# The tensors of a two-block transformer kernel placed in another order in SBUF

## The chip, the cores and the metric

The kernel runs on one core of a Trainium2 chip. The metric is the device time of one execution in microseconds (us); the median of three is 3204.19 us.

## The reference

Two transformer blocks of two layers each, on a sequence of 256 tokens with model width 2048 (batch 1), in float32. The first block has an even layer (latent attention, blocked causal attention, attention over a memory of 256 rows) and an odd one (windowed attention, dilated attention, memory attention). The second has two layers that each run a top-k sparse attention, a gated causal convolution of width 31 over 1024 channels, and a stick-breaking attention, merged by gates. Every layer has the same frame, in which nearly all multiplications lie:

```python
h = rms_norm(x, norm_g) @ w_in            # 256 x 2048 by 2048 x (some 7,000 to 18,064)
...
x = x + (y * silu(gate)) @ w_out          # block 1; block 2: x + merged @ w_out
```

After each block x is normalised by rms_norm with a gain. The weights are read once, some 557 MB in all.

## The kernel before

**The weight products.** Every product with a weight matrix is cut into "gemms" of up to 512 output columns, and each gemm into "fills" of 256 rows of the weight. There are 1088 fills. A fill f goes through five steps. SP's queue loads 2 x 512 float32 for each of 128 partitions (512 KB) into `raw[f % 4]`, in pieces of 2048 bytes (step `raw`). ScalarE copies it as float32r (`wh[f % 4]`, step `hi`, line 118). VectorE subtracts that from `raw` and gets the remainder (`wl[f % 4]`, step `lo`, line 121). TensorE multiplies (step `mm`, line 103): the activations lie transposed in a high and a low half (Hh and Hl, or Yh and Yl), and for each of two row blocks and two halves of the tokens it issues three matmuls, high x high, high x low, low x high: twelve per fill. `wh` and `wl` are the moving operand with up to 512 columns, a 128 x 128 piece of H or Y is the stationary one. The sums are in PSUM (`gp`, two buffers), and ScalarE and VectorE take them out.

**The other work.** Attention heads, transposes (`ident` is the identity for them; line 106), softmaxes, the convolution (31 `tap` steps on VectorE per channel block, line 126, reading `glu`, then `mean` and `var` on TensorE with the constant `ones`), and the norms are small steps that run between fills.

**What is placed where.** `place` (line 306) allocates SBUF with a stack. The compiled program of the kernel before starts it at byte 16,512 of each partition and rounds each tensor's length up to 32 bytes. Names that the text uses: X is the residual stream, H and Y the pairs of transposed activations, Z a second pair (`Yh2`, `Yl2`), M (`merged`) the sum of the branches, of which `glu`, `cv` and `csq` of the convolution are parts, G the attention regions (`ones`, `tri`, `kiT` lie at its ends), `nat`, `tmp` and `st` rings of buffers, `cc` the convolution's columns, `gc` (`gcols`) the gains. Y, `mkT` and `mv` are allocated in an `ExitStack` called `first` that ends before Z and M are allocated, so Z and M lie over them: these tensors share bytes, in time one after the other.

**What sets the order.** A planner sketches every step of every engine with an estimated duration from the operation's element count, then builds each engine's order by simulating it: steps become ready when what they wait for is done, rings give buffers, and `urgency` ranks what is ready. The order found is what each engine runs, with waits on semaphores. It is computed when the program is built.

Of the kernel before, what the change touches and what calls it, by code (L numbers as in the profile page):

```python
# [5 lines left out]
F = mybir.dt.float32  # L6
R = mybir.dt.float32r
# [288 lines left out]
class Program:  # L296
# [7 lines left out]
    def sb(self, name, shape, dt=F, ctx=None):  # L304
        return (ctx or self.ctx).enter_context(self.nc.sbuf_tensor(name, shape, dt))

    def place(self):
        nc, sb = self.nc, self.sb
        self.ident = sb("ident", [128, 128])
        self.cc = sb("cc", [128, 272])  # L310
        self.small = sb("small", [128, 64])
        sb("pad", [128, 16])
        self.X = sb("X", [128, 2, 2048])
        H = (sb("Hh", [128, 16, 256], R), sb("Hl", [128, 16, 256], R))
        self.raw = [sb(f"raw{i}", [128, 2, 512]) for i in range(RAW)]
        self.wh = [sb(f"wh{i}", [128, 2, 512], R) for i in range(SPLIT)]
        self.wl = [sb(f"wl{i}", [128, 2, 512], R) for i in range(SPLIT)]
        self.G = sb("G", [128, 2, 4608])
        self.nat = Ring(self.plan, [sb(f"nat{i}", [128, 2, 512])[:] for i in range(2)])
        self.tab = sb("tab", [128, 2, 256])  # L320
        self.tmp = Ring(self.plan, [sb(f"tmp{i}", [128, 512])[:] for i in range(5)])
        with ExitStack() as first:
            Y = (sb("Yh", [128, 20, 256], R, first), sb("Yl", [128, 20, 256], R, first))
            self.mkT = sb("mkT", [128, 1024], F, first)
            self.mv = sb("mv", [128, 2, 512], F, first)
        Z = (sb("Yh2", [128, 16, 256], R), sb("Yl2", [128, 16, 256], R))
        self.M = sb("merged", [128, 2, 2048], F)
        self.masks = sb("masks", [128, 3, 384])
        self.gcols = sb("gc", [128, 102])
        self.st = Ring(self.plan, [sb(f"st{i}", [128, 8])[:] for i in range(10)])  # L330
        self.gp = [self.ctx.enter_context(nc.psum_tensor(f"gp{i}", [128, 2, 512], F)) for i in range(2)]
        banks = [self.ctx.enter_context(nc.psum_tensor(f"bk{i}", [128, 512], F))[:] for i in range(4)]
        self.bank = Ring(self.plan, banks)
        self.pairs = {"H": [H, H, H, Z], "Y": [Y, Y, Z, H]}
        M = self.M[:, :, :].rearrange("p t c -> p (t c)")
        self.glu = M[:, 0:8 * 286].rearrange("p (c t) -> p c t", t=286)
        self.cv = self.glu[:, :, 30:286]
        self.acc_tap = [M[:, 2304:2560], M[:, 2560:2816]]
        self.csq = M[:, 2304:3328].rearrange("p (c t) -> p c t", t=256)
        self.cvar = [M[:, 3584:3840], M[:, 3840:4096], M[:, 2304:2560]]  # L340
        self.region = []
        for i in range(2):
            d = {k: self.G[:, i, 1024 * n:1024 * n + 1024] for n, k in enumerate("qkvg")}
            d["pe"] = self.G[:, i, 4096:4608]
            self.region.append(d)
        g0, g1 = self.region[0]["pe"], self.region[1]["pe"]
        self.memnat = self.G[:, 1, 0:4096].rearrange("p (t c) -> p t c", t=2)
        self.gfin = self.G[:, 0, 0:2048]
        self.kpe = self.cc[:, 0:256]
        self.swk, self.swv = g1, g0  # L350
        self.kiT, self.ones = g1[:, 0:256], g1[:, 288:416]
        self.wi = g1[:, 256:288].rearrange("p (t h) -> p t h", t=2)
        self.work, self.tri = g0[:, 0:384], g0[:, 384:512]
        self.acc, self.strict = self.masks[:, 1, :], self.masks[:, 2, :]
        s = self.small
        self.rs, self.rsh, self.rm, self.rq, self.rk = s[:, 0:2], s[:, 2:4], s[:, 4:6], s[:, 20:22], s[:, 22:24]
        self.sum_x, self.sum_q, self.sum_kv, self.sum_m = s[:, 8:16], s[:, 16:18], s[:, 18:20], s[:, 48:56]
        self.zero = s[:, 40:41]
# [1674 lines left out]
```

How the kernel before makes its waits and increments, by code:

```python
    def wait_ge(self, sem, value):  # L81
        if sem is None:
            return
        if self.e is None:
            self.plan.step.waits += [(sem, k) for k in value]
        elif self.seen.get(id(sem), 0) < value:
            self.e.wait_ge(sem, value)
            self.seen[id(sem)] = value
# [699 lines left out]
    def load_mem2():  # L788
        e.wait_ge(*P.p_in.at(("y", 3, 2)))
        e.dma_start(P.memnat, m).then_inc(*P.s_mem2.up("mem", 16))
# [1 line left out]
    def raw(f):  # L792
        gm, j = P.fills[f]
        if f:
            e.behind("raw", f - 1)
        else:
            e.behind("load_mem", 3)
        if f == RAW:
            e.behind("load_x", 3)
        if f >= RAW:
            e.wait_ge(*P.v_lo.at(f - RAW))
        elif f == 1:
            e.wait_ge(*P.s_id.at("id"))
            e.wait_ge(*P.s_rows.at(*range(8)))
        k = 256 * j
        src = gm.w[k:k + 256, gm.c0:gm.c0 + gm.n].rearrange("(t p) n -> p t n", p=128)
        e.dma_start(P.raw[f % RAW][:, :, 0:gm.n], src).then_inc(*P.s_raw[f % RAW].up(f, 16))
# [10 lines left out]
    def load_constants():  # L818
        for n in range(4):
            e.wait_ge(*P.s_x[n].at("x"))
        e.dma_start(P.masks[:, :, :], I["c_masks"][0:3].rearrange("m p c -> p m c")).then_inc(*P.s_masks.up("m", 16))
        e.dma_start(P.tab[:, :, :], I["c_tab1"]).then_inc(*P.s_tab.up("t", 16))
        e.dma_start(P.small[:, 24:40], I["od_sinks"].broadcast_to([128, 16])).then_inc(*P.s_sinks.up("s", 16))
# [29 lines left out]
    def pad(l):  # L853
        if l:
            e.wait_ge(*P.p_in.at(("m", 0, 14)))
        else:
```

## Time and profile before

| what | value |
|---|---|
| median of three executions | 3204.19 us (3203.88 to 3207.12) |
| the profiled execution, its own time | 3207.12 us |
| its span, first to last instruction | 3205.3 us |
| mean granted clock of TensorE, as a share of 2.4 GHz | 0.995 |
| TensorE, VectorE, ScalarE busy | 99%, 62%, 50% |
| SP's transfers, share of sixteen DMA engines | 58.2% |
| moved from and to HBM, mean | 176 GB/s |

The profile is of one execution. An engine's busy share is a mean over the span; TensorE's is made of matmuls whose ends are modelled, so two that follow one another overlap in it, and the time of one step is the distance between two starts. The chain that ended last goes back from the last instruction to what released each one, and says whose time the span is made of.

### The profile page before, as it was taken

Reading aid. Unit: us, or ns where it says so; the run is one execution under the profiler, and the core shown is the slowest. Engines: PE = TensorE matmul, PEld = TensorE weight load, DVE = VectorE, ACT = ScalarE, POOL = GpSimd, SP = SyncE. Lnnn points to the kernel's source line nnn. Section 1 sums busy time; section 2 is a strip of 40 time slices with the busy share of each in tenths; the row PEclk is TensorE's granted clock in tenths of the full one; section 3 lists DMA queues with packets and bytes.
Section 4 is the critical chain, followed back from the end, with each engine's and each line's share of the span. In section 5 each row is a group of like instructions: output and inputs, shape, how many; then the busy total and the mean of one; then the engine's idle time right before and its main releaser. Section 6 shows DMA issues by size and latency. Waiting matters only on the chain.

```text
span 3205.3 us, 38474 instructions
## 1 busy us (share of the span) xinstructions
PE 3164.4 (99%) x15199; PEld 2656.7 (83%) x15199; DVE 1981.0 (62%) x2987; ACT 1600.4 (50%) x2254; POOL 14.2 (0%) x30
## 2 busy tenths in 40 slices
PE   8999999999999899999999999999999999999997
PEld 7888888888988788888888888888888888888886
DVE  5555455555554699976554555558999655555554
ACT  6654454555554544556544444454454645444443
POOL 0000000000000000000000000000000000000000
PEclk9999999999999999999999999999999999999999
DMA  6546656555466555555566666566555566666664
GB/s 230 173 135 173 171 194 185 177 156 154 143 191 205 153 179 164 166 156 165 170 191 191 188 196 194 181 188 177 168 171 164 152 177 179 195 201 194 193 186 140
DMA packets 300559, 566.14 MB, mean 177 GB/s; under 512 B 18088, under 2 KB 36814, under 8 KB 299868
## 3 DMA queue, kind: packets, MB, share of 16 engines
q1 hardware_dynamic: 298384, 557.65, 58.2%
q0 software_dynamic: 1648, 5.92, 0.5%
q8 instruction: 120, 1.97, 0.3%
q14 instruction: 59, 0.48, 0.0%
q10 hardware_dynamic: 348, 0.12, 0.0%
HBM read 561.52 MB, written 2.10 MB: 176 GB/s over the span
## 4 chain that ended last, share of the span: by engine, by line
PE 98%; DVE 1%; ACT 1%; ACTq 0%; issue 0%; DMA 0%; POOL 0%; DVEq 0%
PE gp L103 90%; PE bk L103 5%; PE bk L106 3%; DVE X L126 0%; ACT bk L118 0%; ACTq L162 0%; DMA tmp<-in_conv_ln_b 0%; ACT L115 0%; DVE X L121 0%; POOL tmp L162 0%; DVE Yl L126 0%; ACT gp L118 0%; DVE tmp L138 0%; DVE wl L121 0%; ACT G L118 0%
## 5 line engine op out<-in xcount | busy, mean ns | idle before, releaser
L121 DVE TENSOR_TENSOR wl<-raw,wh 128x1024 fp32r<-128x1024 f32 (+3 forms) x1088 | 1287.5, 1187 | 955.7 <-ACT wh L118 954.3
L118 ACT ACTIVATE wh<-raw 128x1024 fp32r<-128x1024 f32 (+3 forms) x1088 | 1119.7, 1032 | 1347.0 <-PE gp L103 1338.8
L103 PE MATMUL gp<-wh,Hh 128*128 128x512 f32 (+3 forms) x2400 | 926.3, 386 | 0.1
L103 PE MATMUL gp<-wh,Hl 128*128 128x512 f32 (+3 forms) x2400 | 912.6, 380 | 0.0
L103 PE MATMUL gp<-wl,Hh 128*128 128x512 f32 (+3 forms) x2400 | 911.9, 380 | 0.0
L103 PE MATMUL gp<-wh,Yh 128*128 128x512 f32 (+2 forms) x1952 | 763.1, 391 | 0.0
L103 PE MATMUL gp<-wh,Yl 128*128 128x512 f32 (+2 forms) x1952 | 755.5, 387 | 0.0
L103 PE MATMUL gp<-wl,Yh 128*128 128x512 f32 (+2 forms) x1952 | 755.3, 387 | 0.0
L103 PEld LDWEIGHTS gp<-wh,Hl 128*128 128x128 f32 x2400 | 451.7, 188 | 86.5
L103 PEld LDWEIGHTS gp<-wh,Hh 128*128 128x128 f32 x2400 | 452.2, 188 | 82.7 <-issue 1.3
L103 PEld LDWEIGHTS gp<-wl,Hh 128*128 128x128 f32 x2400 | 452.3, 188 | 81.4
L103 PEld LDWEIGHTS gp<-wh,Yl 128*128 128x128 f32 x1952 | 367.1, 188 | 74.6
L103 PEld LDWEIGHTS gp<-wl,Yh 128*128 128x128 f32 x1952 | 367.5, 188 | 71.7
L103 PEld LDWEIGHTS gp<-wh,Yh 128*128 128x128 f32 x1952 | 367.4, 188 | 71.3
L126 DVE SCALAR_TENSOR_TENSOR merged<-merged,cc 128x256 f32<-128x256 f32 x480 | 202.0, 478 | 0.0
L118 ACT ACTIVATE nat<-gp,small 128x512 f32<-128x512 f32 (+3 forms) x228 | 133.9, 632 | 136.3 <-PE gp L103 136.1
L103 PE MATMUL bk<-G 128*128 128x128 f32 (+3 forms) x408 | 73.8, 333 | 0.3 <-DVE st L138 0.2
L103 PEld LDWEIGHTS bk<-G 128*128 128x128 f32 (+1 forms) x408 | 59.9, 189 | 10.9 <-issue 3.0
L118 ACT ACTIVATE tmp<-tmp,st 128x128 f32<-128x128 f32 (+1 forms) x124 | 55.8, 451 | 18.5 <-DVE st L132 18.5
L118 ACT ACTIVATE tmp<-bk 128x384 f32<-128x384 f32 (+1 forms) x110 | 50.8, 494 | 25.2 <-PE bk L106 22.7
L103 PEld LDWEIGHTS bk<-G,tmp 128*128 128x128 f32 x420 | 52.8, 191 | 2.7
L103 PE MATMUL bk<-G,tmp 128*128 128x128 f32 (+1 forms) x420 | 53.0, 273 | 0.0
(118 smaller groups left out, 1247.7 us busy)
## 6 DMA issues: line engine op xcount, KB each, us to landing
raw<-in_w_in SPq DMA_DIRECT2D x560, 512.0 KB, 3.8
raw<-in_ev_w_in SPq DMA_DIRECT2D x104, 512.0 KB, 3.8
raw<-in_od_w_in SPq DMA_DIRECT2D x80, 512.0 KB, 3.7
raw<-in_w_out SPq DMA_DIRECT2D x64, 512.0 KB, 4.0
raw<-in_ev_w_out SPq DMA_DIRECT2D x40, 512.0 KB, 3.6
raw<-in_od_w_out SPq DMA_DIRECT2D x36, 512.0 KB, 4.3
raw<-in_w_b_out SPq DMA_DIRECT2D x32, 512.0 KB, 4.8
raw<-in_w_a_out SPq DMA_DIRECT2D x32, 512.0 KB, 4.8
```

Of the source, the lines that this page charges most:

```text
L103: return self.e.matmul(out, l, r, start=start, stop=stop)
L106: return self.sketch(112) if self.e is None else self.e.transpose(out, in_, ident)
L118: return self.e.activation(out, in_, func, **kw)
L121: return self.sketch(157 + size(a) * 1.042) if self.e is None else self.e.tensor_tensor(out, a, b, op)
L126: return self.e.scalar_tensor_tensor(out=out, in0=a, scalar=s, in1=b, op0=op0, op1=op1)
```

## The change

The change is in `place` alone. It allocates the same tensors in another order and leaves out `pad`, 64 bytes that nothing uses. X comes first; `ident`, `cc`, `small` and `tab` go behind the rings, with `st`, `masks` and `gc` that stood at the end; Z and M get an `ExitStack` of their own, `second`, after which nothing is allocated. The PSUM tensors are allocated before `first` instead of at the end, in their old order.

```diff
     def place(self):
         nc, sb = self.nc, self.sb
-        self.ident = sb("ident", [128, 128])
-        self.cc = sb("cc", [128, 272])
-        self.small = sb("small", [128, 64])
-        sb("pad", [128, 16])
         self.X = sb("X", [128, 2, 2048])
...
         self.nat = Ring(self.plan, [sb(f"nat{i}", [128, 2, 512])[:] for i in range(2)])
+        self.tmp = Ring(self.plan, [sb(f"tmp{i}", [128, 512])[:] for i in range(5)])
+        self.st = Ring(self.plan, [sb(f"st{i}", [128, 8])[:] for i in range(10)])
+        self.ident = sb("ident", [128, 128])
+        self.masks = sb("masks", [128, 3, 384])
+        self.gcols = sb("gc", [128, 102])
+        self.cc = sb("cc", [128, 272])
         self.tab = sb("tab", [128, 2, 256])
-        self.tmp = Ring(self.plan, [sb(f"tmp{i}", [128, 512])[:] for i in range(5)])
+        self.small = sb("small", [128, 64])
+        self.gp = [self.ctx.enter_context(nc.psum_tensor(f"gp{i}", [128, 2, 512], F)) for i in range(2)]
+        banks = [self.ctx.enter_context(nc.psum_tensor(f"bk{i}", [128, 512], F))[:] for i in range(4)]
+        self.bank = Ring(self.plan, banks)
         with ExitStack() as first:
             Y = (sb("Yh", [128, 20, 256], R, first), sb("Yl", [128, 20, 256], R, first))
             self.mkT = sb("mkT", [128, 1024], F, first)
             self.mv = sb("mv", [128, 2, 512], F, first)
-        Z = (sb("Yh2", [128, 16, 256], R), sb("Yl2", [128, 16, 256], R))
-        self.M = sb("merged", [128, 2, 2048], F)
-        self.masks = sb("masks", [128, 3, 384])
-        self.gcols = sb("gc", [128, 102])
-        self.st = Ring(self.plan, [sb(f"st{i}", [128, 8])[:] for i in range(10)])
-        self.gp = [self.ctx.enter_context(nc.psum_tensor(f"gp{i}", [128, 2, 512], F)) for i in range(2)]
-        banks = [self.ctx.enter_context(nc.psum_tensor(f"bk{i}", [128, 512], F))[:] for i in range(4)]
-        self.bank = Ring(self.plan, banks)
+        with ExitStack() as second:
+            Z = (sb("Yh2", [128, 16, 256], R, second), sb("Yl2", [128, 16, 256], R, second))
+            self.M = sb("merged", [128, 2, 2048], F, second)
```

The first byte of each tensor in a partition, worked out from the lengths:

| tensor | bytes | start before | start after |
|---|---|---|---|
| X | 16,384 | 18,432 = 9 x 2048 | 16,512 = 8 x 2048 + 128 |
| Hh, Hl | 2 x 16,384 | 34,816 = 17 x 2048 | 32,896 = 16 x 2048 + 128 |
| raw, wh, wl | 4 x 4096 each | 67,584; 83,968; 100,352 | 65,664; 82,048; 98,432 |
| G | 36,864 | 116,736 = 57 x 2048 | 114,816 = 56 x 2048 + 128 |
| nat, tmp | 2 x 4096, 5 x 2048 | 153,600; 163,840 | 151,680; 159,872 |
| ident | 512 | 16,512 | 170,432 |
| cc | 1088 | 17,024 | 175,968 |
| tab | 2048 | 161,792 | 177,056 |
| Yh (and Z over it) | 20,480 | 174,080 = 85 x 2048 | 179,360 = 1401 x 128 + 32 |
| M | 16,384 | 206,848 = 101 x 2048 | 212,128 = 1657 x 128 + 32 |
| masks | 4608 | 223,232 | 170,944 |

## Rows read from the trace of the kernel before

**Rows 1.** The page, parts 1 and 3: busy us, share, instructions; the SP queue.
```profile
PE 3164.4 (99%) x15199; PEld 2656.7 (83%) x15199; DVE 1981.0 (62%) x2987; ACT 1600.4 (50%) x2254; POOL 14.2 (0%) x30
...
q1 hardware_dynamic: 298384, 557.65, 58.2%
```

**Rows 2.** The page, part 4: the chain that ended last, by engine and line.
```profile
PE 98%; DVE 1%; ACT 1%; ACTq 0%; issue 0%; DMA 0%; POOL 0%; DVEq 0%
PE gp L103 90%; PE bk L103 5%; PE bk L106 3%; DVE X L126 0%; ACT bk L118 0%; ACTq L162 0%; DMA tmp<-in_conv_ln_b 0%; ACT L115 0%; DVE X L121 0%; POOL tmp L162 0%; DVE Yl L126 0%; ACT gp L118 0%; DVE tmp L138 0%; DVE wl L121 0%; ACT G L118 0%
```

**Rows 3.** The same chain in order of time: start, us, what, instructions.
```profile
959.55 87.07 PE gp L103 x384
...
1774.29 250.26 PE gp L103 x1104
```

**Rows 4.** Timeline of TensorE at 1000 us: start, duration, what.
```profile
1000.21 0.39 PE L103 MATMUL gp<-wh,Yh 128*128 128x512 f32 x1
...
1000.89 0.39 PE L103 MATMUL gp<-wh,Yh 128*128 128x512 f32 x1
```

**Rows 5.** Groups by line: busy us, mean ns of one, idle before.
```profile
L103 PE MATMUL gp<-wh,Hh 128*128 128x512 f32 (+3 forms) x2400 | 926.3, 386 | 0.1
...
L103 PE MATMUL gp<-wh,Yh 128*128 128x512 f32 (+2 forms) x1952 | 763.1, 391 | 0.0
...
L103 PEld LDWEIGHTS gp<-wh,Yh 128*128 128x128 f32 x1952 | 367.4, 188 | 71.3
```

**Rows 6.** Timeline of TensorE: first the mean, then the variance's first half.
```profile
1421.59 3.62 PE L103 MATMUL bk<-merged,G 128*128 128x256 f32 x16
...
1430.53 1.89 PE L103 MATMUL bk<-merged,G 128*128 128x256 f32 x8
```

**Rows 7.** Timeline of TensorE in a gemm of 256 columns.
```profile
625.06 0.28 PE L103 MATMUL gp<-wh,Hh 128*128 128x256 f32 x1
625.18 0.28 PE L103 MATMUL gp<-wl,Hh 128*128 128x256 f32 x1
```

**Rows 8.** Groups of weight loads by form: busy us, mean ns, idle before.
```profile
L103 PEld LDWEIGHTS bk<-merged,G 128*128 128x128 f32 x64 | 12.1, 189 | 1.9
...
L103 PEld LDWEIGHTS bk<-cc,G 64*128 64x128 f32 x32 | 4.7, 184 | 3.6 <-issue 2.7
```

**Rows 9.** Line 126 on VectorE: duration ns min/median/max, first and last start.
```profile
L126 DVE SCALAR_TENSOR_TENSOR merged<-merged,cc x480: 464/478/491, 1115.5 to 2482.8; 128x256 f32<-128x256 f32 x160
...
L126 DVE SCALAR_TENSOR_TENSOR Hl<-bk,gc,Hh x48: 472/476/484, 36.0 to 1071.0; 128x256 fp32r<-128x256 f32 x48
```

**Rows 10.** Busy us per stretch: span, PE, PEld, DVE, ACT, POOL; clock, DMA, GB/s.
```profile
2200.00:2500.00 300.00, 300.00 (x1480) 253.77 (x1479) 269.30 (x539) 147.25 (x216) 0.00 (x0) 1.00 0.57 168
```

**Rows 11.** DMA from 1774 to 2024 us: queue (packets, MB, share); issues, us to landing.
```profile
q1 hardware_dynamic: 24809, 47.83, 64.7%
...
raw<-in_w_in SPq DMA_DIRECT2D x56, 512.0 KB, 4.3
...
raw<-in_w_c_out SPq DMA_DIRECT2D x16, 512.0 KB, 5.0
```

**Rows 12.** Waits: engine, line, for what, us in total, times, longest.
```profile
PE bk L106 <- DMA ident<-in_c_ident: 10.6, 1, 10.6
...
ACT wh L118 <- DMA raw<-in_od_w_in: 4.9, 5, 2.0
...
PEld gp L103 <- DVE wl L121: 0.3, 1, 0.3
```

**Rows 13.** Busy us of the first 20 us, columns as in rows 10.
```profile
0.00:20.00 20.00, 7.08 (x27) 6.11 (x28) 6.58 (x16) 14.38 (x33) 0.29 (x5) 1.00 0.83 280
```

**Rows 14.** Busy us in the pause between the blocks, columns as in rows 10.
```profile
1050.00:1055.00 5.00, 1.11 (x5) 1.12 (x6) 3.40 (x9) 2.45 (x6) 0.00 (x0) 0.50 0.38 107
```

**Rows 15.** The chain at the pause's end: start, us, what.
```profile
1059.83 4.46 PE gp L103 x12
```

## The prediction

> **What bounds the kernel now.** I read the page first. TensorE is busy in 99% of the span, VectorE in 62%, and SP's transfers take 58.2% of sixteen DMA engines [rows 1]. A busy share of TensorE proves little alone, since the ends of its matmuls are modelled, so the chain that ended last comes next: 98% of it is TensorE, 90% the one line that issues the split matmuls of the weight products, and VectorE and ScalarE have 1% each [rows 2]. The time is the sum of TensorE's own steps.
>
> How long is one such step? The chain has a stretch of 1104 matmuls and nothing else in 250.26 us: 0.2267 us each; one some 800 us earlier has 384 in 87.07 us, again 0.2267 us [rows 3]. The timeline shows it from start to start: three steps from 1000.21 to 1000.89 [rows 4]. The long stretch runs through all raw and split slots many times, with transfers landing and ScalarE and VectorE reading and writing beside it, and its mean is that of the short one. So other engines' accesses don't slow TensorE's reads today, and new addresses can only change the step itself, or make something else late enough to be waited for.
>
> The groups give the count: 2400 matmuls with H and 1952 with Y, each in three kinds, 3 x 2400 + 3 x 1952 = 13,056 [rows 5]. Most have 512 columns.
>
> **The change, part by part.** It touches no instruction, size, loop, ring or wait. The planner orders steps by names, element counts and ring slots; no address enters it, the rings keep their lengths, and PSUM is laid out as before. Tensors that shared bytes (Z and M over Y, mkT and mv) share the same bytes relative to each other, so no new overlap wants a new wait. The order on each engine stays, and what differs is the byte at which each tensor starts. Five things could cost something.
>
> (1) *Matmuls.* wh, wl and H move from multiples of 2048 bytes to 128 bytes past a multiple of 256. Does TensorE care where a moving operand starts? No row has the split matmul at another kind of start. The nearest is in the convolution. Its mean reads `cv`, whose rows start 120 + 1144c bytes into M, at a different place in a 64-byte block for each of the eight c; its variance reads `csq`, on a multiple of 1024. The mean's 16 passes take 3.62 us, the variance's 8 take 1.89 us [rows 6]. Less the last pass's 0.38 us that is 3.24 / 15 = 0.216 us and 1.51 / 7 = 0.216 us from start to start: odd starts cost nothing that shows. But such a pass of 256 columns takes 0.216 / 256 = 0.84 ns per column, and the split matmul takes 0.120 us for 256 [rows 7], so (0.2267 - 0.120) / 256 = 0.417 ns per column: it reads twice as fast, and the row is near but not the thing itself. I take 0. Upper bound: one column time for each, 13,056 x 0.417 ns = +5.4 us. Lower bound: the same with the other sign, as 0.2267 us is 512 x 0.417 = 0.213 us and 13 ns of fixed part, and nothing proves that no part of it comes from today's starts.
>
> The Trainium skill ("SBUF — State Buffer", Specifications) says that SBUF has lines of 16 bytes and that each crossing to a new one costs something. By that rule the sum stays as well, as every tensor starts on such a line before and after; the mean's operands, half of which start 8 bytes past one, are where this trace could have shown the cost, and 0.216 us against 0.216 us doesn't show it.
>
> (2) *Weight loads from Y and Z.* These move from multiples of 512 to 32 bytes past a multiple of 128. A load takes 188 ns and the next matmul starts 227 ns after the last [rows 5, 4]: 39 ns of cover. The mean's loads, from `ones` at 128 past a multiple of 512, take 189 ns, and those from half the rows 184 ns [rows 8]. With 1 to 4 ns between forms and 39 ns of cover I take 0 for both bounds; without cover 1 ns on each of 5856 would be +6 us.
>
> (3) *VectorE and ScalarE* read and write Y, Z and M at 32 past a multiple of 64. The 480 convolution taps read `glu` at a start that moves by 4 bytes per tap and last 464 to 491 ns, median 478; the same operation and size into Hl, always on a round start, 476 [rows 9]. Were each 13 ns longer (the maximum less the median), that is 6.2 us of VectorE for both layers. In the tightest stretch, 2200 to 2500 us, it is busy for 269 of 300 us while TensorE is busy for all 300 [rows 10]: 31 us of cover for one layer's half. Without cover, +6.2 us. I take 0.
>
> (4) *Weight transfers.* Each 2048-byte piece of `raw` starts 128 past a multiple of 256. In the long stretch SP's transfers occupy 64.7% of the engines for 47.83 MB, 91.2 tiles of 512 KB: 0.647 x 250 / 91.2 = 1.77 us per tile [rows 11], against 12 x 0.2267 = 2.72 us of TensorE. A tile has to become 1.53 times dearer before transfers set the pace. Latency is covered too: `lo` frees the raw slot of tile f - 4 about 2.3 us (ScalarE's 1.06, VectorE's 1.22) after TensorE is done with f - 8, and `hi` can take tile f only once TensorE is done with f - 4. That leaves 4 x 2.72 - 2.3 = 8.6 us for a landing of 4.3 to 5.0 us [rows 11]. ScalarE waits 4.9 us in all for the worst group of raw tiles, and TensorE's loads wait for `lo` 0.3 us [rows 12]. If it had no cover, each 1% on a tile would be 18 ns on 1016 full ones, 18 us. I take 0.
>
> The Trainium skill ("DMA: Bandwidth & Descriptors", How a descriptor splits into AXI transactions) says that transfers are made of transactions that begin at multiples of 256 bytes, so that a descriptor off such a multiple needs one more. It speaks against this change. By it 2048 bytes would take 9 instead of 8, an estimate of 1.77 x 9 / 8 = 2.0 us per tile, still under 2.72, and the sum would be the same; no row of before can show it.
>
> (5) *Start and end.* Only here are transfers close to the bound: they are 0.83 busy in the first 20 us [rows 13], and TensorE waits for ident until 10.6 us [rows 12]. If they got a tenth dearer (my choice) and nothing hid it, the start would be 2 us later, and the last stores a little. I take 0, with 0 and +2 us as bounds.
>
> **Sum.** The profiled execution took 3207.12 us, its span 3205.3 us, so 1.8 us lie around it. 3207.12 + 0 (five times) = 3207.1 us. It is the slowest of the three executions, 2.9 us (0.09%) above their median of 3204.19, so as a median I forecast **3204.2 us**. About 0.2%, 6.4 us, is what a measurement of this kernel can tell from no change.
>
> **Rivals.**
> *The split matmul does mind its start.* For it: no row has it at another start, and it is 90% of the chain. Against: rows 6. With four column times more on each, 13,056 x 1.67 ns = +21.8 us: **3226 us**. It decides from 6.4 / 13,056 = 0.49 ns per matmul on, little more than one column time.
> *Transfers become the bound.* If a tile took twice its time, 3.54 us against 2.72: 0.82 x 1016 = +830 us, **4037 us**. It decides from a factor of 1.53 on. Against it: rows 11; nothing in the trace shows a transfer that slows by so much.
> *The old starts were the worse ones.* Place: the 13 ns of fixed part. With four column times less, 3204.2 - 21.8 = **3182 us**. For it only that the fixed part is there; against it rows 6. It decides from -0.49 ns on.
> *The half clock moves.* After TensorE's pause at 1046.6 us its granted clock is 0.50 of 2.4 GHz, the lower level of 1.2 GHz [rows 14], and twelve matmuls take 4.46 us instead of 2.72 [rows 15]. The pause is a chain of ScalarE and VectorE steps that stays. Without the lower clock some 2 us would come back: **3202 us**, which lies within no change.
>
> **How the numbers follow.** Within 0.2%: 0.88, of which 0.86 is my forecast and 0.02 the half clock. Slower by more: 0.09, of which 0.07 is the matmul that minds its start and 0.02 transfers. Faster by more: 0.03, the old starts. Range: up +5.4 for the column time, +2 for the start and 1.4 for the part of the slow matmul's case just above, giving 3213; down 2 us for the clock and 1 for scatter (the runs lie from 3203.88 to 3207.12), giving 3201. I leave out the full -5.4 us, for which nothing speaks but symmetry. Less than 0.15 is left outside.
>
> **What would show each step right or wrong.** Right: the same number of instructions, the chain at 98% TensorE, long stretches of L103 at 0.2267 us per matmul. (1) is wrong if that quotient is 0.2272 or more, or 0.2262 or less. (2) is wrong if loads from Yh or Yl take over 200 ns while those from Hh keep 188. (3) would show in the taps' 478 ns. (4) would show in SP's share of the DMA engines, 58.2%, and matters only if ScalarE's waits for raw grow past some 10 us. (5) would show in the start of the first weight product. The prediction fails as a whole if the order of steps changed, or if the split matmul's step depends on where its operand starts.

## The result and the profile after

The changed kernel takes 3240.84 us in the median of four executions, beside 3204.69 us for the kernel before on the same chip: a ratio of 1.0111 (95% interval 1.0099 to 1.0124), 36 us or 1.1% slower. I had forecast 3204.2 us and no change; the time lies outside my range of 3201 to 3213 us.

The page of the changed kernel, parts 1 and 4:

```profile
span 3240.7 us, 38474 instructions
...
PE 3199.1 (99%) x15199; PEld 2657.2 (82%) x15199; DVE 1982.5 (61%) x2987; ACT 1601.1 (49%) x2254; POOL 14.2 (0%) x30
...
PE 98%; DVE 1%; DMA 0%; ACT 0%; issue 0%; POOL 0%; SPq 0%; DVEq 0%
```

The counts are those of before, VectorE's and ScalarE's busy times moved by 1.5 and 0.7 us, and TensorE still has 98% of the chain [rows 1, 2]. The matmuls of the two traces follow one another with the same names and forms, all 15,199 of them. So the same steps run in the same order, and TensorE's own steps got longer. Which ones, the chain in order of time tells:

```profile
286.80 29.94 PE gp L103 x132
...
964.83 89.61 PE gp L103 x384
...
1782.91 252.65 PE gp L103 x1104
...
2866.12 255.34 PE gp L103 x1104
```

The first stretch has H as its stationary operand: 29.94 / 132 = 0.2268 us per matmul, the old step. The second has Y: 89.61 / 384 = 0.2334 us, where it was 0.2267 [rows 3]. The two long ones show it again. In the third layer (1782.91) 348 of the matmuls have Z as stationary operand and are slow: 252.65 - 250.26 = 2.4 us is 6.9 ns for each. In the fourth (2866.12) the roles are exchanged, H's lines run on Z, and the other 756 are slow: 5.1 us, 6.7 ns each. So it goes by the bytes from which the stationary operand is read, and the moving operand's new start, which all stretches share, costs nothing.

The groups by form give the count and the sum:

```profile
L103 PE MATMUL gp<-wh,Hh 128*128 128x512 f32 x2176 | 861.4, 396 | 0.0
...
L103 PE MATMUL gp<-wh,Yh 128*128 128x512 f32 x1888 | 754.8, 400 | 0.0
...
L103 PE MATMUL gp<-wh,Yl 128*128 128x384 f32 x32 | 10.8, 336 | 0.0
```

Matmuls of 512 columns with a Y or Z piece: 3 x 1888 = 5664. 5664 x (0.2334 - 0.2268) = 37 us, against a loss of 36 us. The trace's own loads of these pieces didn't get longer: they take 188 ns as before [rows 5].

```profile
L103 PEld LDWEIGHTS gp<-wh,Yh 128*128 128x128 f32 x1952 | 367.6, 188 | 82.4
```

Only the idle time ahead of them grew, from 71.3 to 82.4 us for this kind. And the convolution's mean, which was my measure of an odd start, takes 3.62 us as in [rows 6], although M moved too.

```profile
1428.80 3.62 PE L103 MATMUL bk<-merged,G 128*128 128x256 f32 x16
```

### The profile page after: what moved, and what is told of

Same layout as the page of the kernel before. It is cut to its first block, busy times and chain, and to the rows that moved or that the text cites. A ratio compares the mean times of both kernels' runs of the same rounds, so it can differ in the third digit from the quotient of the medians.

```text
span 3240.7 us, 38474 instructions
## 1 busy us (share of the span) xinstructions
PE 3199.1 (99%) x15199; PEld 2657.2 (82%) x15199; DVE 1982.5 (61%) x2987; ACT 1601.1 (49%) x2254; POOL 14.2 (0%) x30
## 3 DMA queue, kind: packets, MB, share of 16 engines
q1 hardware_dynamic: 298384, 557.65, 57.3%
## 4 chain that ended last, share of the span: by engine, by line
PE 98%; DVE 1%; DMA 0%; ACT 0%; issue 0%; POOL 0%; SPq 0%; DVEq 0%
PE gp L103 90%; PE bk L103 5%; PE bk L106 3%; DVE X L126 0%; DMA G<-in_mem 0%; DMA tmp<-in_conv_ln_b 0%; ACT L115 0%; DVE X L121 0%; POOL tmp L162 0%; DVE Yl L126 0%; ACT gp L118 0%; DVE tmp L138 0%; ACT bk L118 0%; SPq L162 0%; DVE wl L121 0%
## 5 line engine op out<-in xcount | busy, mean ns | idle before, releaser
L103 PE MATMUL gp<-wh,Yh 128*128 128x512 f32 (+2 forms) x1952 | 774.4, 397 | 0.0
L103 PE MATMUL gp<-wh,Yl 128*128 128x512 f32 (+2 forms) x1952 | 766.9, 393 | 0.0
L103 PE MATMUL gp<-wl,Yh 128*128 128x512 f32 (+2 forms) x1952 | 766.8, 393 | 0.0
L103 PEld LDWEIGHTS gp<-wh,Yh 128*128 128x128 f32 x1952 | 367.6, 188 | 82.4
```

The source lines that it names most:

```text
L103: return self.e.matmul(out, l, r, start=start, stop=stop)
```

## The experiments

Each is an edit of one of the two kernels that adds unused bytes. "Distance" is the stationary operand's first byte (H or Y) less the moving one's (wh), modulo 256. It is 0 for both in the kernel before, and H 0, Y 32 in the changed one (179,360 - 82,048 = 97,312 = 380 x 256 + 32). For offsets it is enough to look at the first bytes: wh and wl, the halves of H, Y and Z, and the pieces within them all lie multiples of 256 bytes apart, unless a run says otherwise. Every ratio is to the kernel before, measured beside it.

### Y alone, 32 bytes further

```diff
+        sb("pad_y", [128, 8])
         with ExitStack() as first:
```

> The kernel before with 32 unused bytes ahead of Yh: only Y, mkT, mv, Z, M, masks, gc and st move, by 32 bytes, and all else stays. Theory A (TensorE's stationary operand must start on a multiple of 64 bytes, absolutely): each of the 5664 matmuls of 512 columns with a stationary Y or Z piece takes 0.2333 us instead of 0.2267, +36 us, about 3241 us. Theory B (what counts is the distance between the starts of the moving and the stationary operand): Y stands at 32 from wh's multiple of 64, so +36 us as well. Theory C (the order of the other tensors, ident, cc, tab or masks, or the 128 bytes of H, wh and raw cause it): no change, 3204 us.

Measured: 3239.99 us, ratio 1.0107 (1.0091 to 1.0122).

```profile
285.74 29.94 PE gp L103 x132
...
963.84 89.62 PE gp L103 x384
```

H 0.2268 us, Y 0.2334 us: the whole loss, from moving Y and what lies behind it by 32 bytes in the kernel before. Theory C falls: neither the new order of the small tensors nor the 128 bytes of wh, H and raw have a part in it.

### All big tensors 32 bytes further

```diff
-        sb("pad", [128, 16])
+        sb("pad", [128, 24])
```

> The kernel before with the pad made 96 bytes instead of 64: every tensor from X on moves by 32 bytes, so H, Y, Z, wh, wl and raw all start 32 bytes past a multiple of 2048 and keep their distances. Theory A (absolute start of the stationary operand): all 12,192 matmuls of 512 columns pay 6.4 ns, +78 us, about 3282 us, and H's step is 0.233 us too. Theory B (distance of the two operands): no change, 3204 us, all steps 0.2267 us. Theory C: no change in the steps either.

Measured: 3206.07 us, ratio 1.000 (0.9991 to 1.0010).

```profile
958.55 87.07 PE gp L103 x384
```

Y again starts 32 past a multiple of 2048, as in the run above, and takes 0.2267 us. Theory A, which blames the start itself, falls, and the distance is left. The run also answers for every other reader and writer at once: with X, raw, wh, wl, G, Y and M all 32 bytes off, transfers, VectorE and ScalarE cost nothing that shows.

### The moving operand alone

```diff
+        sb("pad_w", [128, 8])
         self.wh = [sb(f"wh{i}", [128, 2, 512], R) for i in range(SPLIT)]
         self.wl = [sb(f"wl{i}", [128, 2, 512], R) for i in range(SPLIT)]
+        sb("pad_g", [128, 8])
         self.G = sb("G", [128, 2, 4608])
```

> The kernel before with 32 unused bytes ahead of wh and 32 behind wl: only wh and wl, the moving operand, start 32 bytes past a multiple of 64; H, Y and Z stay on multiples of 2048; G and what follows moves by 64 bytes. Theory A (only the stationary operand's start counts): no change, 3204 us. Theory B (distance of the two): both H and Y are now 32 bytes off, +78 us, about 3282 us. A third, D (any operand that is off 64 bytes costs it): +78 us as well; all32 parts B from D.

One sentence of this was inexact: Y and Z move with G by 64 bytes, so that Y stands at +32 from wh, and H at -32 (224 modulo 256). Both are off, as the expectation wants it. Measured: 3275.98 us, ratio 1.0218 (1.0203 to 1.0233).

```profile
288.92 30.79 PE gp L103 x132
...
974.69 89.61 PE gp L103 x384
```

0.2333 and 0.2334 us: now H is as slow as Y. 12,192 x 6.5 ns would be +79 us, and +70 were measured. Part of the gap comes from fills that stand alone between other work: in the changed kernel the chain has one of twelve matmuls with Y in 2.80 us against 2.74 before, 5 ns each instead of 6.6. Together with the run before this is theory B. It also speaks against other pairs: Y keeps its distance from G and the rings, which moved with it, and is slow; H keeps its distance from raw and X and is slow. What moved against both of them is wh and wl.

### How long is the unit

Y in the changed kernel 32 bytes further, so that 64 divides the distance:

```diff
+        sb("pad_y", [128, 8])
         with ExitStack() as first:
```

> The changed kernel with 32 unused bytes ahead of Yh: Y, Z and M start on a multiple of 64 bytes (179,392 = 2803 x 64) and everything else is as in the changed kernel. Theories A and B: the whole loss comes back, 3204 to 3206 us, and Y's step is 0.2267 us again (in A as 64 divides the start, in B as the distance to wh, 97,344, is 1521 x 64). Theory C: no change against the changed kernel, 3241 us.

Measured: 3241.16 us, 1.0110 (1.0095 to 1.0126). Theories A and B had expected the loss back. Y's stretch is no better, so 64 isn't the unit.

```profile
964.18 89.62 PE gp L103 x384
```

So I took two distances per kernel, one for H and one for Y:

```diff
+        sb("pad_r", [128, 16])
         self.raw = [sb(f"raw{i}", [128, 2, 512]) for i in range(RAW)]
...
+        sb("pad_y", [128, 32])
         with ExitStack() as first:
```

> The kernel before with 64 unused bytes ahead of raw and 128 ahead of Yh. Distances of the stationary from the moving operand's start, modulo 2048: H at -64, Y at +128. Theory B (the distance matters), with three sizes of the unit that must divide it. B128: H slow (0.2333 us, 6528 x 6.2 ns = +40 us), Y not (0.2267): 3246 us. B256 or more: both slow, +40 + 35 us, 3281 us. Rival F (only distances below some limit, such as 128, are in each other's way, whatever divides them): H slow, Y not, 3246 us; the next kernel parts it from B128.

Measured: 3248.33 us, 1.0133 (1.0118 to 1.0148).

```profile
286.78 30.23 PE gp L103 x132
...
966.38 89.23 PE gp L103 x384
```

H at -64: 0.2290 us, a third of the usual loss, which neither theory had. Y at +128: 0.2324 us, slow, so B128 and F with its limit of 128 fall. With 64 floats ahead of raw and 128 ahead of Yh:

> The kernel before with 256 unused bytes ahead of raw and 512 ahead of Yh: H at -256, Y at +512 from the moving operand, modulo 2048. B with a unit of 256 or less, and F: no change, 3206 us, all steps 0.2267. B512: H slow, Y not, 3246 us. B with 1024 or 2048: both slow, 3281 us.

Measured: 3205.50 us, 0.9998 (0.9988 to 1.0007), both stretches as in the kernel before:

```profile
283.10 29.94 PE gp L103 x132
...
956.65 87.07 PE gp L103 x384
```

If the cost has a unit, it divides 256 and doesn't divide 128, so it is 256. Rival F with a limit of up to 256 would fit these two runs as well; against it stands the changed kernel, whose Y lies 97,312 = 47 x 2048 + 1056 bytes from wh, far from a multiple of 2048, and pays the same 0.2334 us as Y at +32. Then the changed kernel with 56 floats ahead of Yh, which makes the distance 381 x 256:

> The changed kernel with 224 unused bytes ahead of Yh: Y, Z and M move from 97,312 = 380 x 256 + 32 to 97,536 = 381 x 256 bytes behind wh, and nothing else moves. Theory P256 (the step of the split matmul depends on the distance between the stationary and the moving operand's start modulo 256 bytes, and a multiple of 256 is the undisturbed case): the whole loss comes back, 3205 to 3207 us, with H and Y at 0.2267 us. If the unit is 512 or more (the distance is an odd multiple of 256 here): no change against the changed kernel, 3241 us.

Measured: 3206.44 us, 1.0002 (0.9992 to 1.0012).

```profile
284.82 29.94 PE gp L103 x132
...
958.36 87.07 PE gp L103 x384
```

224 unused bytes give the changed kernel its 36 us back, at an odd multiple of 256. It equals the kernel before and doesn't beat it.

### Is it a period, and what lies between

24 floats ahead of raw and 64 ahead of Yh; 32 and 24; 56 and 48:

> The kernel before with 96 unused bytes ahead of raw and 256 ahead of Yh: H at -96, which is 160 modulo 256, and Y at +256 from the moving operand. P256: Y stays at 0.2267 us, H is slow by an amount between those of 128 (0.2326) and 192 (0.2293), about 0.231 us: 6528 x 4 ns = +28 us, 3234 us. Unit of 512: Y is slow as well, +35 us more, 3269 us.

> The kernel before with 128 unused bytes ahead of raw and 96 ahead of Yh: H at -128, Y at +96. P256: -128 and +128 are the same, so H takes the 0.2326 us that Y took at +128, +39 us, and Y takes 0.233 us, +35 us: 3280 us. Rival S (the sign counts and negative distances cost less, as -64 did with 0.2293 us against 0.2333 us at +64): H takes 0.229 us or less, +15 us, 3256 us.

> The kernel before with 224 unused bytes ahead of raw and 192 ahead of Yh: H at -224, which is +32 modulo 256, and Y at +192, which is -64. P256: H takes the 0.2333 us of +32, +43 us, and Y the 0.2293 us of -64, +15 us: 3264 us. Rival S (sign and size count, no period): H at a large negative distance takes 0.229 us or less and Y at a large positive one 0.2326 us: +15 + 33 us, 3254 us, with the slow and the less slow side exchanged in the trace.

Measured: 3245.33 us, 1.0124 (1.0109 to 1.0139); 3277.49 us, 1.0223 (1.0208 to 1.0238); 3255.95 us, 1.0155 (1.0140 to 1.0171). Their stretches, H's and then Y's, one fence for each:

```profile
287.95 30.80 PE gp L103 x132
...
970.86 87.07 PE gp L103 x384
```

```profile
288.69 30.67 PE gp L103 x132
...
974.67 89.98 PE gp L103 x384
```

```profile
288.08 30.80 PE gp L103 x132
...
971.44 87.93 PE gp L103 x384
```

H at -128 takes 0.2323 us and Y at +128 had 0.2324. H at -224 takes 0.2333 and Y at +32 had 0.2334. Y at +192 takes 0.2290 and H at -64 had 0.2290. Three pairs agree that are 256 bytes apart and on opposite sides. The third carries most, since +64 took 0.2334 us: neither the sign nor the size of a distance gives 0.2290 at both -64 and +192, and a period does. In the last kernel H is the slow side and Y the less slow one, as P256 wants and rival S doesn't. Its time, 3256 us, is nearer S's 3254 than P256's 3264. But a step from a long stretch, multiplied by all matmuls, comes out too high, as it did in the run with wh and wl moved, so the steps themselves decide. The interpolation for -96 was wrong: 0.2333 us, where I had put 0.231, so that run took 3245 and not 3234 us.

### Sixteen bytes, and one of the two moving operands

wh and wl cut out of one tensor at 16 bytes past its start:

```diff
-        self.wh = [sb(f"wh{i}", [128, 2, 512], R) for i in range(SPLIT)]
-        self.wl = [sb(f"wl{i}", [128, 2, 512], R) for i in range(SPLIT)]
+        both = sb("whl", [128, 2048 * SPLIT + 4], R)
+        slots = [both[:, 4 + 1024 * i:1028 + 1024 * i].rearrange("p (k c) -> p k c", k=2) for i in range(2 * SPLIT)]
+        self.wh, self.wl = slots[:SPLIT], slots[SPLIT:]
```

> The kernel before with wh and wl cut out of one tensor at 16 bytes past a multiple of 2048, which moves G and all behind it by 32 bytes: H at -16, Y at +16. If the two streams cost each other anything as soon as their starts differ, both steps are 0.2333 us, 3281 us. If only a distance of 32 bytes or more counts (a line or a pair of lines of 16 bytes), both stay at 0.2267, 3206 us. If the sign counts, one of H and Y is slow and the other not, 3241 or 3246 us.

Measured: 3273.84 us, 1.0211 (1.0196 to 1.0227).

```profile
288.86 30.57 PE gp L103 x132
...
973.55 90.88 PE gp L103 x384
```

0.2316 us for H at -16 and 0.2367 us for Y at +16, the slowest step of all: a distance of 16 bytes is not too small to count. But Y's step is not fixed by the distance. By these two quotients the run would be 6528 x 4.8 ns + 5664 x 9.9 ns = 87 us longer, and it is 68. The fourth layer's long stretch, 756 of whose matmuls have Z at +16, takes only 252.53 us beside 250.26 before. It begins at 0.2333 us per step (15 in 3.50 us from 2899.97) and goes on, in the same execution, at 0.2267 us (nine in 2.04 us from 3000.03), the step of the kernel before.

```profile
2898.97 252.53 PE gp L103 x1104
```

The durations show it too, first in the stretch with Y, then late in the one with Z:

```profile
L103 PE MATMUL gp<-whl,Yh x238: 398/400/474, 964.7 to 1049.6; 128*128 128x512 f32 x119
...
L103 PE MATMUL gp<-whl,Yh x24: 388/388/388, 3000.0 to 3007.7; 128*128 128x512 f32 x24
```

By the starts in the trace about a sixth of the steps with Y or Z in this run pay nothing, a tenth some 6.6 ns and most 10 ns, in blocks of tens to hundreds of us. A distance of 192 does it more rarely. In the run with H at -224 and Y at +192 two neighbouring stretches with Y take 0.2333 and 0.2291 us:

```profile
2602.43 22.40 PE gp L103 x96
...
2625.71 21.99 PE gp L103 x96
```

What switches the step from one value to another, no run here shows.

32 unused bytes ahead of wl only:

```diff
+        sb("pad_l", [128, 8])
         self.wl = [sb(f"wl{i}", [128, 2, 512], R) for i in range(SPLIT)]
```

> The kernel before with 32 unused bytes ahead of wl: H at 0 from wh and -32 from wl; Y at +32 from wh and 0 from wl. The three matmuls of a product follow as (high, wh), (high, wl), (low, wh). Theory B, with the cost at each matmul whose moving operand is off the stationary piece that is loaded meanwhile: with H only the matmul on wl is slow, 2176 x 6.2 ns = +13 us; with Y the two on wh, 3776 x 6.2 ns = +23 us; together +37 us, 3243 us, and the trace shows the slow steps on those alone. Rival G (it is the jump from one moving operand's start to the next one's that costs): with both H and Y two of three starts follow a jump, and both are slow alike, +50 us, 3256 us.

Measured: 3270.02 us, 1.0199 (1.0184 to 1.0214), more than either theory gives. Durations in a stretch with H, min, median and max in ns, beside a median of 389 for all three matmuls in the kernel before:

```profile
L103 PE MATMUL gp<-wh,Hl x41: 393/393/393, 289.6 to 317.6; 128*128 128x512 f32 x41
L103 PE MATMUL gp<-wh,Hh x41: 395/395/395, 289.9 to 317.9; 128*128 128x512 f32 x41
L103 PE MATMUL gp<-wl,Hh x40: 400/400/400, 290.1 to 317.4; 128*128 128x512 f32 x40
```

The ends are modelled, but the mean excess, (4 + 6 + 11) / 3 = 7 ns, is that of the steps (30.79 / 132 = 0.2333 us). The matmul on wl pays most, and the two on wh, whose start is in line with H, pay as well. With Y it is the other way round: wl is in line with it and wh isn't, and the matmul on wl pays least.

```profile
L103 PE MATMUL gp<-wl,Yh x121: 391/393/397, 964.7 to 1049.5; 128*128 128x512 f32 x121
L103 PE MATMUL gp<-wh,Yl x121: 391/397/397, 964.9 to 1049.8; 128*128 128x512 f32 x121
```

So both theories missed the size, and G, in which H and Y behave alike, the place too. To see whose pair counts, the last run moves only the low half of the stationary operand, and not the whole:

```diff
-            Y = (sb("Yh", [128, 20, 256], R, first), sb("Yl", [128, 20, 256], R, first))
+            Y = [sb("Yh", [128, 20, 256], R, first)]
+            sb("pad_l", [128, 8], F, first)
+            Y.append(sb("Yl", [128, 20, 256], R, first))
```

and the same between the halves of Z.

> The kernel before with 32 unused bytes between Yh and Yl, and between the two halves of Z: Yh stays on a multiple of 2048 bytes from wh, Yl and Z's low half stand at +32. The three matmuls of a product are (Yh, wh), (Yh, wl), (Yl, wh). O (the cost is at the matmul whose own stationary piece is off): one of three steps is slow, the one from (Yl, wh) to the next, 1888 x 6.4 ns = +12 us, 3217 us. N (the load of the next stationary piece runs beside the moving read, and that pair counts): also one of three and the same time, but the slow step is the one from (Yh, wl) to (Yl, wh). M (one piece out of line disturbs the two streams for the matmuls that follow, as the steps with both starts in line were slow too where only wl had moved): all three steps are slow, +36 us, 3241 us.

Measured: 3238.33 us, 1.0100 (1.0083 to 1.0117).

```profile
L103 PE MATMUL gp<-wl,Yh x122: 397/400/400, 964.8 to 1049.5; 128*128 128x512 f32 x122
L103 PE MATMUL gp<-wh,Yl x122: 389/389/389, 965.0 to 1049.7; 128*128 128x512 f32 x122
L103 PE MATMUL gp<-wh,Yh x122: 395/395/395, 965.2 to 1049.9; 128*128 128x512 f32 x122
```

The time is M's. These durations are modelled, and their excesses, 6, 11 and 0 ns, don't add up to the step's; the starts in the trace do. In this stretch the next matmul starts 232 ns after (Yh, wh), 239 after (Yh, wl) and 229 after (Yl, wh), beside 226, 227 and 227 in the kernel before. The matmul whose own stationary piece is the one out of line, (Yl, wh), pays least, 2 ns; the one ahead of it, (Yh, wl), beside which Yl is loaded, pays most, 12 ns; and (Yh, wh) pays 6. So O falls. N has the place of the largest share right and the sum wrong, M has the sum right, but not equal shares.

## Why the prediction was wrong, point by point

**What bounds the kernel, and what the change does: right.** The order on each engine, the counts and the 98% stayed, and only TensorE's own step was left to change. I had even named its quotient, 0.2272 us or more, as the sign of failure; it is 0.2334 us, for Y.

**Step (1), "does TensorE care where a moving operand starts?": the question that failed.** The answer I gave to it, 0, is right: H's steps with wh 128 bytes off stay at 0.2268 us, and with all tensors 32 bytes off everything does. What the runs showed in its place: the step depends on where the two operands start relative to each other. All of H, Y, wh and wl lay at multiples of 2048, so every pair in the trace of before was in line and no row could show the effect. That the step was the same all through the stretches of [rows 3], which I read as a sign that TensorE's reads meet nobody else's, held for other engines' accesses and said nothing of TensorE's two own streams.

**The row I leaned on was the wrong kind.** [Rows 6] have two distances too, and still 0.216 us each. They are the slow kind of pass, at 0.84 ns per column, with 256 columns. The effect doesn't appear there after the change either. It was called "near but not the thing itself", and then given 0.88 of the weight.

**The size.** The upper bound of (1) was one column time per matmul, +5.4 us, a guess with no row behind it. Measured are 6.6 ns, 16 column times of 0.417 ns, on the 5664 with Y: 37 us. The rival that the split matmul minds its start had the right place and sign, at four column times on all 13,056, +21.8 us. It had a chance of 0.07.

**Step (2), weight loads from Y: 0 was wrong in effect, right in its own row.** I costed them against 39 ns of cover by their own duration, which is 188 ns still. That they run beside the moving read is what costs, as far as the run with Yl alone moved can tell, and the "load over 200 ns" that I named as the sign would never have shown it.

The Trainium skill ("SBUF — State Buffer", Who interferes with whom) gives TensorE two read ports, one for the moving operand and one for weight loads, and calls them independent. These runs speak against that for matmuls of 512 columns: with the same instructions, moving Y and what lies behind it by 32 bytes makes the steps with Y 6.6 ns longer. By the 16-byte lines of the Trainium skill (the same page, Specifications), which I had weighed, every one of these layouts would be as fast as the old one; the one with wh and wl at 16 bytes past is 2.1% slower.

**Steps (3), (4), (5): shown right.** In the changed kernel the taps last 477 ns in the median (478 before), SP's share is 57.3% of a longer span (about as much time as the 58.2% of before), ScalarE waits 6.1 us for the worst group of raw tiles, and the first weight product ends at 17.69 + 4.79 = 22.5 us, beside 17.85 + 4.88 = 22.7 before:

```profile
L126 DVE SCALAR_TENSOR_TENSOR merged<-merged,cc x480: 461/477/483, 1122.7 to 2502.5; 128x256 f32<-128x256 f32 x160
```

```profile
q1 hardware_dynamic: 298384, 557.65, 57.3%
```

The extra transaction that by the Trainium skill ("DMA: Bandwidth & Descriptors", How a descriptor splits into AXI transactions) a piece off a multiple of 256 bytes costs doesn't show on the SBUF side, which is the side that moved, either at 128 or at 32 bytes past: SP's share is 58.3% with everything 32 bytes off. The run with everything 32 bytes off bounds all three together: ratio 1.000, within 0.1%.

**The other rivals.** Transfers as the bound and the old starts as the worse ones didn't occur; no distance of the ten tried gave 512 columns in less than 0.2267 us.

**What stays open.** That the two streams meet is argued from which steps are slow and from the last run, not seen. What switches the step between values at one and the same distance, most of all at 16 bytes, why the excess spreads over the matmuls that follow, why a distance of 64 bytes forwards costs 6.6 ns and 64 backwards 2.2, and why 256 bytes are the unit, these runs don't say.

## What to carry to other kernels

When a kernel is bound by matmuls of 512 columns that each have another stationary piece loaded beside them, the two operands' addresses are a tuning knob: here the long stretches kept their 0.2267 us wherever the two starts differed by a multiple of 256 bytes, and a reordering of allocations that broke this cost 1.1%, two broken pairs 2.2%. Compute the first byte of every operand before and after a change of layout, and compare the distances between those read together, not only each one's alignment. A step that is the same all through a trace proves that nothing varies, not that nothing is paid; where the trace has only one kind of layout, give the other kind a wide range.

## What the runs showed of the hardware that was not expected

Steps of the 512-column split matmul by the distance of stationary from moving operand, from the stretches above (0: all stretches; the others: one or two). In other stretches the step at 16 also takes 0.2267 and 0.2333 us, and at 192 also 0.2333 us, so these two rows are what the stretches shown took and not constants:

| distance modulo 256, bytes | step, us | excess, ns |
|---|---|---|
| 0 | 0.2268 | 0 |
| 16 | 0.2367 | 10 |
| 32, 64 | 0.2334 | 6.6 |
| 96 | 0.2343 | 7.5 |
| 128 | 0.2324 | 5.6 |
| 160 | 0.2333 | 6.5 |
| 192 | 0.2290 | 2.2 |
| 224 | 0.2333 | 6.5 |
| 240 | 0.2316 | 4.8 |

For narrower matmuls it is another matter. With 384 columns, Y at 32 costs nothing: 336 ns in the changed kernel's group by form and 335 before. At 16 it does cost, by the durations of the run with wh and wl at 16 bytes:

```profile
L103 PE MATMUL gp<-whl,Yl 128*128 128x384 f32 x32 | 11.0, 343 | 0.0
```

With 256 columns and H at 224 the step is even a little shorter, in the run that moves wh and wl:

```profile
632.76 0.28 PE L103 MATMUL gp<-wh,Hl 128*128 128x256 f32 x1
...
633.82 0.28 PE L103 MATMUL gp<-wh,Hl 128*128 128x256 f32 x1
```

Nine steps in 1.06 us are 0.118 us each, beside 0.120 us in [rows 7]. There are only 480 of these, so nothing is to be won by it here.
